# Own buffer and own DMA queue for the modulation quarters of a two-block transformer kernel, and a new order of its last stick-breaking round

## The reference

```python
mod = silu(c) @ w_ada + b_ada              # 6 x 1024 values from one vector c
h = modulate(rms_norm(x, g_mix), shift, scale)
# w_in gives q, k, v for 8 softmax heads ("moba"), q, k, v for 8 stick-breaking
# heads ("sb"), and two gates of width 1024
o_moba = softmax(q k^T / 8 + rel_bias, causal) v
z = q k^T / 8                              # stick breaking
log_keep = where(past, log_sigmoid(-z), 0)
a = where(past, exp(log_sigmoid(z) + cumsum_of_later(log_keep)), 0);  o_sb = a v
mixed = sigmoid(gate0) * (o_moba @ w_br_moba) + sigmoid(gate1) * (o_sb @ w_br_sb)
x = x + gate_row * (mixed @ w_out)
```

## Time and profile before

| | us |
|---|---|
| median of 3 runs (1547.39 to 1549.16) | 1547.57 |
| the profiled execution, its own time | 1547.21 |
| its span, first to last instruction | 1545.5 |
| TensorE, matmuls | 1464.2 busy |
| VectorE | 927.2 busy |
| ScalarE | 734.3 busy |
| GpSimd | 57.8 busy |

### The profile page before, as it was taken

One profiled execution on the slowest core, in us unless ns is written; L12 is line 12 of the kernel. 1 busy time (PEld: TensorE's weight loads), 2 busy tenths in 40 slices (PEclk: granted clock), 3 DMA queues, 4 the chain that ended last, 5 costly groups with the idle time before them and its releaser, 6 DMA issues.

```text
span 1545.5 us, 17969 instructions
## 1 busy us (share of the span) xinstructions
PE 1464.2 (95%) x6791; PEld 1199.3 (78%) x6791; DVE 927.2 (60%) x1128; ACT 734.3 (48%) x990; POOL 57.8 (4%) x104
## 2 busy tenths in 40 slices
PE   5999988999998999999789999999999999999998
PEld 5777767778887888877567888878888778788886
DVE  5675667588875654467955654556454455565443
ACT  1555544545654544355444644445444465564441
POOL 2000000000000000022100000000000100000000
PEclk9998989999999999999879999999999999999999
DMA  8964555277652855534214655546555373456540
GB/s 318 322 219 147 206 178 184 77 258 252 203 206 73 267 178 186 183 120 147 82 55 151 222 187 192 189 150 218 190 191 191 123 211 110 136 172 223 181 173 28
DMA packets 180310, 274.29 MB, mean 177 GB/s; under 512 B 6241, under 2 KB 120673, under 8 KB 180225
## 3 DMA queue, kind: packets, MB, share of 16 engines
q1 hardware_dynamic: 176976, 263.45, 50.5%
q0 software_dynamic: 1824, 6.57, 1.4%
q10 hardware_dynamic: 1425, 3.12, 0.7%
HBM read 272.05 MB, written 1.06 MB: 177 GB/s over the span
## 4 chain that ended last, share of the span: by engine, by line
PE 77%; DVE 11%; ACT 4%; issue 4%; DMA 2%; POOL 0%; DVEq 0%; SPq 0%; POOLq 0%; ACTq 0%
PE psum L2039 23%; PE psum L2041 23%; PE psum L2040 23%; DVE w_lo L1661 3%; ACT w_hi L1474 2%; PE psum L2234 2%; DMA raw<-in_w_ada_dram 1%; PE psum L2110 1%; DVE ada_acc L1702 1%; PE psum L2163 1%; PE psum L2162 1%; DVE PR L1978 1%; PE psum L2178 1%; DVE scr L2001 1%; DMA raw<-in_w_in_dram 1%
## 5 line engine op out<-in xcount | busy, mean ns | idle before, releaser
L1661 DVE TENSOR_TENSOR w_lo<-raw,w_hi 128x2048 fp32r<-128x2048 f32 x157 | 358.2, 2286 | 191.1 <-ACT w_hi L1474 187.7
L2039 PE MATMUL psum<-w_hi,hT_hi 128*128 128x512 f32 x1000 | 401.4, 401 | 14.1 <-DVE w_lo L1661 4.4
L2041 PE MATMUL psum<-w_hi,hT_lo 128*128 128x512 f32 x1000 | 392.5, 393 | 0.0
L2040 PE MATMUL psum<-w_lo,hT_hi 128*128 128x512 f32 x1000 | 391.7, 392 | 0.0
L1474 ACT ACTIVATE w_hi<-raw 128x2048 fp32r<-128x2048 f32 x157 | 299.3, 1908 | 167.4 <-PE psum L2041 101.1
L2039 PEld LDWEIGHTS psum<-w_hi,hT_hi 128*128 128x128 f32 x1000 | 190.0, 190 | 62.2 <-issue 18.6
L2041 PEld LDWEIGHTS psum<-w_hi,hT_lo 128*128 128x128 f32 x1000 | 189.4, 189 | 40.8
L2040 PEld LDWEIGHTS psum<-w_lo,hT_hi 128*128 128x128 f32 x1000 | 190.2, 190 | 36.7
L1661 DVE TENSOR_TENSOR lo_qk<-raw,hi_qk 128x2048 fp32r<-128x2048 f32 (+1 forms) x35 | 79.2, 2264 | 41.9 <-ACT hi_qk L1474 41.9
L2039 PE MATMUL psum<-w_hi,hc_hi 128*128 128x512 f32 x256 | 101.0, 395 | 1.8 <-DVE hc_lo L1666 1.1
L1661 DVE TENSOR_TENSOR lo_at<-raw,hi_at 128x2048 fp32r<-128x2048 f32 x35 | 80.2, 2290 | 35.7 <-ACT hi_at L1474 35.7
(11 more groups left out here) (197 smaller groups left out, 2017.2 us busy)
## 6 DMA issues: line engine op xcount, KB each, us to landing
raw<-in_ffn_wg_dram SPq DMA_DIRECT2D x88, 512.0 KB, 3.7
raw<-in_ffn_wu_dram SPq DMA_DIRECT2D x88, 512.0 KB, 4.7
raw<-in_ffn_wd_dram SPq DMA_DIRECT2D x44, 1024.0 KB, 4.8
raw<-in_w_ada_dram SPq DMA_DIRECT2D x24, 1024.0 KB, 5.5
raw<-in_w_up_dram SPq DMA_DIRECT2D x44, 512.0 KB, 4.8
raw<-in_w_in_dram SPq DMA_DIRECT2D x20, 1024.0 KB, 5.7
raw<-in_even_w_in_dram SPq DMA_DIRECT2D x12, 1024.0 KB, 4.9
raw<-in_odd_w_in_dram SPq DMA_DIRECT2D x12, 1024.0 KB, 5.1
```

The source lines that it names most:

```text
L1661: nc.vector.tensor_tensor(lo_of(s), raw_of(s), hi_of(s).bitcast(F32), ALU.subtract).then_inc(lo_ready, 1)
L2039: nc.tensor.matmul(o, a_hi, b_hi, start=start, stop=False)
L2040: nc.tensor.matmul(o, a_hi, b_lo, start=False, stop=False)
L2041: return nc.tensor.matmul(o, a_lo, b_hi, start=False, stop=stop)
```

## The change

Twelve quarters (n = 4 to 9) no longer pass through the ring. They get one buffer of 8 KB a partition, `ada_raw`, laid over `hc_hi` and `hc_lo`, and GpSimd issues their loads: the first in the step `late_loads`, once the quarters of n = 0 to 3 are used, each further one in the `ada` step of the one before it, once VectorE has used that. The sum of n now comes behind the second part of n + 1, not behind its first. The quarters' places move: one more before the softmax loop; in it behind the second units (i = 1, 3, 5), then at i = 7 and i = 9; one, not two, in stick-breaking round 0.

The transposes of the moba output move from round 4 into round 3, ahead of that round's value products, in banks 2 and 3. Unit 20 moves ahead of the last cumulative sums, three quarters of unit 21 ahead of the last value products, its last quarter between these and the transposes of the sb output; unit 22 follows those directly. Units 21 and 22 use other banks.

```diff
 def load_order(self):
-            elif kind == "ada":
+            elif kind == "ada" and a["own"] is None:
...
-    def ada(n, part, shared=None):
+    def ada(n, part, shared=None, own=False):
...
+        if own:
+            pl.ada_own.append((u, n_ada[0]))
+        pl.add("ada", n=n, part=part, unit=u, done=n_ada[0], tiles=2 if shared else 4, slot_free=sum_uses[n - 2] if n >= 2 else None,
+               own=len(pl.ada_own) - 1 if own else None)
...
     def sum_next(bank=3):
         if sum_due:
-            adasum(sum_due.pop(), bank)
+            adasum(sum_due.pop(0), bank)
 
     def ada_next(bank=3):
 
         n, part = later_ada.pop(0)
-        ada(n, part)
-        sum_next(bank)
+        ada(n, part, own=True)
         if part:
+            sum_next(bank)
             sum_due.append(n)
...
     r["va"] = now(w_in_chunk(2, 2 * BANK, "plain"))
     turns_of("ka", 1, 4, 2, ("uses", r["ka"]))
+    ada_next()
...
-        fa += [[first, ada_next], [second]]
+        fa += [[first], [second, ada_next]]
     fa.append([lambda: turns_of("qb", 3, 8, 6, ("uses", r["qb"])), lambda: turns_of("kb", 4, 12, 6, ("uses", r["kb"]))])
-    fa += [[ada_next], [ada_next]]
+    fa += [[ada_next], [], [ada_next]]
...
-        fb += [[first], [second], [ada_next] if i else [ada_next, ada_next]]
+        fb += [[first], [second], [ada_next]]
...
     def turn_moba():
-        turn("scr", ("uses", moba_out), None, None, 0, 4, (6, 7), GM)
+        turn("scr", ("uses", moba_out), None, None, 0, 4, (2, 3), GM)
...
-    fb += [[turn_moba], [second_branch]]
+    first_part = []
+
+    def first_branch():
+        ya[0], part = branch("w_br_moba", 0, 0, (6, 7), GM)
+        first_part.append(part)
+        pl.split_ahead(part["unit"])
+        product_step("proj", part, ks=(0, 1, 2), inc=None)
+
+    fb[10].append(turn_moba)
+    fb += [[second_branch], [first_branch]]
     o = sb_heads(fb, 5 * BANK, q_ready_of("qb", "kb"), r["vb"])
     o_evac(o, ("scr", BANK), True)
     v = n_scr[0]
-    ya[0], part = branch("w_br_moba", 0, 0, (2, 3), GM)
-    pl.split_ahead(part["unit"])
-    product_step("proj", part, ks=(0, 1), inc=None)
+    product_step("proj", first_part[0], ks=(3,))
     turn("scr", ("scr_ready", v), None, None, 4, 4, (0, 1), GM)
-    product_step("proj", part, ks=(2, 3))
-    yb[0], part = branch("w_br_sb", 0, 4, (6, 7), GM)
+    yb[0], part = branch("w_br_sb", 0, 4, (2, 3), GM)
...
+        ada_raw = nc.alloc_sbuf_tensor_at("ada_raw", [P, UNIT], F32, offset=nc.sbuf_base - 4 * UNIT)
...
+            def load_own(i):
+                nk, w, parts = ada_units[plan.ada_own[i][0]]
+                view = ada_raw[:, :].rearrange("p (k n) -> p k n", k=nk)
+                pool.dma_start(view, parts[0][2]).then_inc(ada_landed, 16)
...
+                elif kind == "late_loads":
+                    pool.wait_ge(ada_used, plan.ada_own[0][1] - 1)
+                    load_own(0)
+                elif kind == "ada":
+                    if a["own"] is not None and a["own"] + 1 < len(plan.ada_own):
+                        pool.wait_ge(ada_used, a["done"])
+                        load_own(a["own"] + 1)
...
-                    dve.wait_ge(weight_loaded[raw_slot[what]], landed[what])
+                    if a["own"] is None:
+                        rows_in = raw[:, raw_slot[what], :]
+                        dve.wait_ge(weight_loaded[raw_slot[what]], landed[what])
+                    else:
+                        rows_in = ada_raw[:, :]
+                        dve.wait_ge(ada_landed, 16 * (a["own"] + 1))
```

More of the change, by code:

```diff
@@ L131, in __init__ @@
         self.steps, self.units, self.ada_units = [], [], []
-        self.ada_done = []
+        self.ada_done, self.ada_own = [], []
         self.tenant, self.announced, self.evacuated = [None] * 8, [0] * 8, [0] * 8
@@ L290, in ada_unit @@
         return len(pl.ada_units) - 1
-    def ada(n, part, shared=None):
+    def ada(n, part, shared=None, own=False):
         n_ada[0] += 1
         u = ada_unit(n, part, shared or n_ada[0])
-        pl.add("ada", n=n, part=part, unit=u, done=n_ada[0], tiles=2 if shared else 4, slot_free=sum_uses[n - 2] if n >= 2 else None)
+        if own:
+            pl.ada_own.append((u, n_ada[0]))
+        pl.add("ada", n=n, part=part, unit=u, done=n_ada[0], tiles=2 if shared else 4, slot_free=sum_uses[n - 2] if n >= 2 else None,
+               own=len(pl.ada_own) - 1 if own else None)
     def adasum(n, bank=None, shared=None):
@@ L1227, in program @@
         small_loaded, bucket_loaded, gate_bias_loaded = sem("small_loaded"), sem("bucket_loaded"), sem("gate_bias_loaded")
-        ada_used = sem("ada_used")
+        ada_used, ada_landed = sem("ada_used"), sem("ada_landed")
         c_act_ready = sem("c_act_ready")
@@ L1697, in _ @@
                         kk = 4 * a["part"] + k
-                        w = raw[:, raw_slot[what], k * BANK:(k + 1) * BANK]
+                        w = rows_in[:, k * BANK:(k + 1) * BANK]
                         if kk == 0:
```

## The result

The changed kernel takes 1551.82 us in the median of seven runs (1548.82 to 1554.26), beside 1547.57 for the kernel before on the same chip: ratio 1.0027, interval 1.0015 to 1.0038. It is slower by 4.2 us, where 2.5 us less was forecast. The profiled execution has a span of 1550.1 us and its own time of 1551.82.

What follows compares the result with a forecast made beforehand. VectorE and ScalarE were taken to pace the stick-breaking rounds, not TensorE. Terms +1.3 (head's -0.6 included), -3.1, 0 and -0.7 sum to -2.5 us: 1545.0 us on the median, range 1540.5 to 1550.5.

Steps and rivals of the forecast that it cites:

- The head: 37 to 130 us: w_in loads move up one place, TensorE's 0.60 us wait at 67.21 goes; -0.6, bounds 0 and -1.4.
- Start of round 0: Between head 7 and first z: TensorE's 3.33 us wait goes, VectorE waits for (7,1), landing in 5.1 us; first z +1.3.
- One quarter fewer: Between first and second z: one quarter stands there instead of two, so with its sum -3.1 us.
- Rounds 1 to 3: Later stick-breaking rounds: each still holds a quarter in the same place; 0.
- Last round: Up to unit 22: reordered work after a wait at sum 8 and low clock; 2.5 less 1.8 started early, -0.7 us.
- Late landing: Rival at (7,1): GpSimd's queue delivers in 11.8 us, all behind is 6.7 later; 1551.8 us, chance 0.14.
- TensorE bounds after all: Rival: TensorE's waits are simply removed, 12.2 us behind 134; 1535.4 us, chance 0.08.
- a TensorE that is dense there: Sign that the prediction would be wrong: TensorE dense from 130 to 210 us.
- Clock stays up: Rival in the last round: the clock does not drop after the wait; -5.5, 1542.0 us, chance 0.20.
- Nothing left: Rival: unit 4's load no earlier, low clock lasts 10 us, small waits take the rest; -0.5, 1547.1 us, chance 0.20.
- 4.4, 5.1 and 11.8 us for the landing: Load of (7,1) before round 0: 5.1 us taken for its landing, with 4.4 and 11.8 as bounds.

Runs made afterwards that it cites:

- quarters earlier: Changed kernel with one more quarter in the head, only (7,1) between head 7 and round 0, and sum 6 on bank 6: 1537.86 us, 0.9935 of before.
- the ring in the same places: The kernel of 1537.86 us with its quarters' places kept, but all quarters in the ring loaded by SyncE, no own buffer: 1538.00 us, 0.9935 of before.
- The buffer alone: Changed kernel with the old last round and branch units; own buffer, GpSimd's loads, moved quarters and later sums stay: 1551.49 us, 1.0023 of before.
- the loads by SP: Changed kernel with the loads of the quarters' own buffer issued by SyncE instead of GpSimd: 1551.19 us, 1.0016 of before.

## Why the prediction was wrong

**The head** (-0.6). The 0.60 us at 67.21 is gone, as said, and the wait of 0.84 at 80 stayed: from the first product (42.87 before, 44.15 after, both at 2.4 GHz) to the first mark it is 36.35 us in place of 37.22. That is -0.9; the prediction's other value for the term, 0, did not come out. It holds only where the first product finds the full clock: where it doesn't, the same stretch takes 37.9 us with the buffer (quarters earlier) and 37.4 with the ring in the same places, so the buffer gains nothing. But from the mark to head 7's end it is 1.25 us more, beside a wait of 1.41 at 125.08 for sum 5's evacuation, which the step didn't have; no version changes that sum's bank alone. Together +0.4: off by 1.0 us.

**Start of round 0** (+1.3 at the first z): this step failed. It counted the wait for (7,1) on VectorE, named what stands behind it there, and priced the landing at 5.1 us; measured were 5.6 us from issue to the quarter's start. But it said of TensorE's 3.33 us that after the change "TensorE has no such wait: it goes". TensorE did not wait for a quarter any more; it waited 10.45 us for the bank of the sum, whose evacuation stands behind the quarter on VectorE. The step had moved the sum on TensorE's list and not the evacuation on VectorE's list. From the end of head 7 the first z came 5.4 us later than before (17.5 against 12.1), where the step has 1.9 (1.3 and the head's 0.6): 3.5 too little, 2.9 of them the bank, by the version with sum 6 on bank 6.

The rest of the 3.5 is near what the 0.3 us ahead of GpSimd's issue and a landing of 5.6 for 5.1 come to.

**One quarter fewer** (-3.1): right. First to second z are 14.2 us apart in place of 17.4. **Rounds 1 to 3** (0): right, 17.9 and 17.5 in place of 17.7 and 17.7. From the first product to the fourth z it is 2.6 us more than before, where 1.8 less was forecast; the error, 4.4, is that of the two steps above.

**Last round** (-0.7 of its own). The wait before sum 8 is 3.70 as forecast, sum 8 takes 1.87 (1.84 forecast), TensorE's rows show the lower clock from there for 5.6 us, to 220.9, where 6.1 was forecast, and the last cumulative sums have no wait. Split low of unit 21 ends 3.9 us later than before and unit 22 starts 3.3 later: -0.6. Mechanism and size were right. Another 1 to 2 us were to be had by another bank for sum 8; the step named the bank as what TensorE waits for and didn't ask for another.

The steps with their measured values, +0.4 head, +5.4 z, -3.2 quarter, 0, and -0.3 from the fourth z to the second mark, make +2.3 where the median says +4.2. Without the part ahead of 80 us, which in other profiles starts at the lower clock, it is +3.2. The buffer alone has +3.0 and by its ratio +3.6, the loads by SP +3.4 and +2.5. So the stretch explains the loss to within 1 us from mark to mark, and to within 2 with the part ahead of 80 us; what is left has no row of its own, and its cause is open.

**The rivals.** *Late landing* gives 1551.8, the time that was measured, by a mechanism that didn't happen: the landing took 5.6 us and not 11.8. That the numbers agree is luck. *TensorE bounds after all* fell: TensorE stood longer than before, and the distance of the later z's is the same with TensorE busy throughout and with it idle for 0.9 us. (The prediction took a TensorE that is dense there for a sign of being wrong; in the changed kernel it was dense between the second and third z, and that decided nothing.) *Clock stays up* fell by the window of 215.20. *Nothing left* (1547.1) fell too. Of 4.4, 5.1 and 11.8 us for the landing, 5.1 was the right choice. The buffer with a queue of its own gains nothing over the ring (1537.86 and 1538.00 us), and SP's queue in GpSimd's place gives only 0.7 us at the first z; with this the rule of the Trainium skill agrees, that DMAs interleave on the same 16 engines whichever engine issued them ("DMA: Bandwidth & Descriptors", Issuing engines are not separate DMA queues). The Trainium skill also says, under "Perfetto Trace Analysis", Matmuls, that independent groups of matmuls should rotate through PSUM banks so that the evacuation of one overlaps the next; sum 6 is a small case of it, as one evacuation of 0.16 us held TensorE for 10.45 us, and another bank took the wait off z's line.

## What to carry to other kernels

When a step is moved on one engine, write out its other half on the other engine too: for each tile or bank that it fills, find in whose queue the reader stands, what is ahead of it there, and who needs the bank next. A single buffer whose load is issued when the tile before is used up puts issue and landing (5.6 us here) in the path, with nothing to hide them, wherever two uses stand back to back; before giving a load a buffer or a queue of its own, try the same places with the buffers that are there. Where one engine sets the pace of a stretch, move its filler work into a part of the kernel where another engine has enough to do meanwhile; that was worth more here (10 us) than every other edit.

## What the runs showed of the hardware

A load of 1024 KB into the same buffer took 5.7 us in the median from GpSimd's queue and 5.2 from SP's (twelve of each); the issue rows differ by 0.38 us (0.75 and 0.37). What a wait leaves of the low clock was not the same each time. With 3.70 us before sum 8, as in the changed kernel, sum 8 and the start of unit 20 run at the lower clock for 5.6 us in all. With waits of 0.59 and 1.55 us, sum 8 between them runs at the full clock (1.05 us for 1.87), and the lower clock, from unit 20's start on, lasts 6.1 us with sum 8 alone on bank 6 and 3.4 us with both sums there (3.1 us with the quarters earlier and sum 8 there). The first matmul that is back at the full clock, on TensorE's timeline with sum 8 alone on bank 6 and then with both:

```profile
219.97 0.41 PE L2068 MATMUL psum<-w_hi,hT_lo 128*128 128x512 f32 x1
```

```profile
214.31 0.40 PE L2068 MATMUL psum<-w_hi,hT_lo 128*128 128x512 f32 x1
```

Work at half the clock loses half its time, so the 2.7 us between 6.1 and 3.4 are some 1.3 us lost, an estimate. That is about what the last parts differ by: it is 1.1 us shorter than without bank 6 in the first, and 2.0 and 2.3 in the other two. Why the clock rose sooner in these is open.

The same code behind the second mark, some 1287 us, differed by up to 5 us between profiles, and the first product of the mixer found the lower clock in some profiles and not in others (0.76 and 0.47 us). In the version with (7,1) in the ring it reads:

```profile
42.90 0.76 PE L2066 MATMUL psum<-w_hi,hT_hi 128*128 128x512 f32 x1 [0.56 <-DVE hT_lo L1688]
```
